# Rotary rows of the last attention packed into 128 partitions by POOL's transfers, and the norm's factor of the queries taken into the softmax

## The reference

```
def rmsnorm_2(x, g):
    y = x32 * lax.rsqrt(jnp.mean(x32 * x32, axis=-1, keepdims=True) + RMS_EPS)
    return (y * g.astype(jnp.float32)).astype(x.dtype)

def partial_rope(x, pos):                  # only the first 16 of 64 rows of a head turn
    x1, x2 = x32[..., :half], x32[..., half:ROT_DIM]
    rot = jnp.concatenate([x1 * cos - x2 * sin, x2 * cos + x1 * sin], axis=-1)
    return jnp.concatenate([rot.astype(x.dtype), x[..., ROT_DIM:]], axis=-1)

def swa_attention(q, k, v, sinks):
    s = jnp.einsum('bnqhgd,bnkhd->bnhgqk', qb, kw) * scale
    s = jnp.where(mask[None, :, None, None], s, NEG_INF)
    m = jnp.maximum(jnp.max(s, axis=-1, keepdims=True), sink)
    e = jnp.exp(s - m)
    denom = jnp.sum(e, axis=-1, keepdims=True) + jnp.exp(sink - m)
    o = jnp.einsum('bnhgqk,bnkhd->bqhgd', e / denom, vw)

h = rmsnorm_2(x, norm_g[1]); p = h @ swa_w_in
q, k = partial_rope(q, pos), partial_rope(k, pos)
y = swa_attention(q, k, v, swa_sinks) * silu(gate)
out = rmsnorm_2(x + y @ w_out, final_g)
```

## Time and profile before

| | |
|---|---|
| median of 3 executions | 2113.01 us (2110.41 to 2113.66) |
| profiled execution, its time | 2112.39 us |
| its span, first to last instruction | 2110.6 us |
| mean granted TensorE clock | 0.998 |
| busy: TensorE / VectorE / ScalarE / POOL | 2089.4 / 1618.0 / 1322.4 / 22.0 us |
| stretch of the last attention | from about 1780 us (end of `fo3`) to the end |

### The profile page before, as it was taken

The page is one execution under the profiler, slowest core; times in us unless marked ns, Lnnn a source line. Parts: engine busy times, 40 slices in busy tenths (PEclk is TensorE's granted clock), DMA queues, the critical chain, the costliest instruction groups (busy, mean ns, idle before and its releaser), DMA issues.

```text
span 2110.6 us, 35203 instructions
## 1 busy us (share of the span) xinstructions
PE 2089.4 (99%) x13756; PEld 1824.4 (86%) x13756; DVE 1618.0 (77%) x2935; ACT 1322.4 (63%) x2610; POOL 22.0 (1%) x42
## 2 busy tenths in 40 slices
PE   9999999999999999999999999999999999999998
PEld 8878888888898888888888888888888888988887
DVE  7899866787788888656888867777686777689874
ACT  6866447775676666544666666556566655567764
POOL 0000000000000000000000000000000000100000
PEclk9999999999999999999999999999999999999999
DMA  7544534665455555655555555555555555644464
GB/s 280 173 147 144 169 120 143 224 219 193 160 190 192 196 192 191 197 193 196 191 195 192 194 196 191 190 191 190 198 182 178 171 195 193 213 159 160 160 210 139
DMA packets 108325, 390.94 MB, mean 185 GB/s; under 512 B 12624, under 2 KB 12880, under 8 KB 107392
## 3 DMA queue, kind: packets, MB, share of 16 engines
q1 hardware_dynamic: 105264, 377.34, 54.0%
q0 software_dynamic: 2608, 11.04, 1.5%
q10 hardware_dynamic: 288, 0.32, 0.0%
HBM read 384.36 MB, written 2.13 MB: 183 GB/s over the span
## 4 chain that ended last, share of the span: by engine, by line
PE 91%; DVE 6%; ACT 2%; issue 1%; DMA 0%; SPq 0%; DVEq 0%; ACTq 0%
PE main L597 86%; PE two L597 4%; DVE W L1104 2%; PE two L600 1%; DVE gt L1104 1%; DVE GV L1110 0%; ACT W L1826 0%; ACT L1825 0%; DMA RAW<-ws 0%; ACT PPw L1826 0%; DVE GK L1110 0%; DVE PB L1104 0%; DVE GQ L1110 0%; DVE NTL L1104 0%; PE main L644 0%
## 5 line engine op out<-in xcount | busy, mean ns | idle before, releaser
L597 PE MATMUL main<-A,W 128*128 128x256 f32 (+2 forms) x7200 | 1249.6, 334 | 7.7 <-DVE W L1104 7.3
L1826 ACT ACTIVATE W<-RAW 128x512 fp32r<-128x512 f32 x1416 | 876.7, 627 | 589.6 <-PE main L597 583.7
L597 PEld LDWEIGHTS main<-A,W 128*128 128x128 f32 (+1 forms) x7200 | 1088.5, 188 | 161.6 <-DVE W L1104 10.6
L1104 DVE TENSOR_TENSOR W<-RAW,W 128x512 fp32r<-128x512 f32 x1416 | 956.3, 685 | 354.6 <-ACT W L1826 345.8
L597 PE MATMUL main<-H,W 128*128 128x512 f32 (+1 forms) x1408 | 239.7, 333 | 0.0
L597 PEld LDWEIGHTS main<-H,W 128*128 128x128 f32 x1408 | 212.2, 188 | 27.3
L597 PE MATMUL main<-B,W 128*128 128x512 f32 (+1 forms) x1216 | 197.9, 324 | 0.3 <-DVE B L1104 0.3
L597 PEld LDWEIGHTS main<-B,W 128*128 128x128 f32 x1216 | 177.3, 188 | 20.4 <-issue 0.5
L597 PE MATMUL main<-W,A 128*128 128x512 f32 (+1 forms) x672 | 150.2, 378 | 0.0
L597 PEld LDWEIGHTS main<-W,A 128*128 128x128 f32 x672 | 117.9, 188 | 22.4 <-issue 0.5
L597 PE MATMUL main<-W,B 128*128 128x512 f32 x384 | 88.2, 390 | 0.0
(11 more groups left out here) (329 smaller groups left out, 1359.9 us busy)
## 6 DMA issues: line engine op xcount, KB each, us to landing
RAW<-ws SPq DMA_DIRECT2D x707, 512.0 KB, 3.3
CB<-cscr POOLq DMA_DIRECT2D x4, 1024.0 KB, 5.3
XT<-xT POOLq DMA_DIRECT2D x4, 512.0 KB, 7.6
MS<-memT POOLq DMA_DIRECT2D x4, 512.0 KB, 10.0
xs<-xT SPq DMA_DIRECT2D x7, 256.0 KB, 8.3
out<-YT SPq DMA_DIRECT2D x7, 256.0 KB, 2.5
CST<-cst SPq DMA_DIRECT2D x1, 1272.0 KB, 7.5
VR<-WV POOLq DMA_DIRECT2D x16, 64.0 KB, 4.5
```

What stands on the lines that cost most here:

```text
L597: return e.matmul(o, l, r, start=start, stop=True, skip_group_check=True)
L1104: return e.tensor_tensor(o, a, b, op)
L1826: return e.activation(o, i, f, bias=bias, scale=scale, accum_out=accum)
```

## The change

- The keys (WK) are multiplied by RB in place, like other parts, at slot END["fo3"] + 13 on VectorE. ScalarE's `keys` copies them to KR 16 slots earlier than before (T_WROPE - 10, with T_WROPE one lower).
- The queries are not multiplied by their factor at all. The row maximum of the raw scores is multiplied by RT inside the maximum with the sink (two instructions of two columns in place of one of four, since RT differs by half), and the exponential takes RT as its scale.
- SP's 36 crosswise transfers, the zeroed ROT tiles and the 9 rotary parts of three 128x512 operations go. In their place: for the keys (r = 0) and each group of eight heads (r = 1 to 4) POOL gathers the 16 turning rows of the tiles' eight halves into one tile PQ of 128 partitions by 256 tokens, and the same rows crosswise into PV, by six transfers; VectorE multiplies PQ and PV by new tables and adds, three operations of 128x256; POOL brings PQ back by two transfers. TensorE's scores wait for that (s_rope) instead of rp_done. VectorE's part is at T_WROPE and T_QROPE[g] = END[wq g] + 6; POOL does its own when the semaphores allow, behind `values` in its list.

```diff
+    for r in range(16):
+        for base in (4 * r, 64 + 4 * r):
+            C[base:base + 4] = cos[r % 8]
+            S[base:base + 4] = sin[r % 8] if r >= 8 else -sin[r % 8]
...
-    if form_of(*_x) == "wide" and _x[0][:2] not in ("wo", "dn", "fo", "w2", "wk", "wq"):
+    if form_of(*_x) == "wide" and _x[0][:2] not in ("wo", "dn", "fo", "w2", "wq"):
...
+        elif _x[0] == "wkv":
+            _e = max(_e, END["fo3"] + 13)
...
-T_WROPE = ENDS["wkv", 0] + 17
-T_QROPE = [[ENDS[f"wq{g}", p] + (15 if (g, p) == (2, 1) else 10) for p in range(2)] for g in range(4)]
+T_WROPE = ENDS["wkv", 0] + 16
+T_QROPE = [END[f"wq{g}"] + 6 for g in range(4)]
...
-            def swap(r):
-                src, dst = wide_to(*ROPED[r]), ROT[r % 2]
...
-                for base in (0, 64):
-                    lower, upper = slice(base, base + 8), slice(base + 8, base + 16)
-                    e.dma_start(dst[lower, :, :], src[upper, :, :]).then_inc(s_rot[r % 2], 16)
-                    e.dma_start(dst[upper, :, :], src[lower, :, :]).then_inc(s_rot[r % 2], 16)
...
-                w.wait_ge(rp_done, 2 * g + 3)
+                w.wait_ge(s_rope, 32 * (g + 2))
...
-                    z = tt(h2(mx), h2(mx), bm(sink, 2), ALU.max)
+                    for t in range(2):
+                        m = mx[:, 2 * t:2 * t + 2]
+                        z = stt(m, m, RT[:, t:t + 1], sink, ALU.mult, ALU.max)
...
-            def rope(key, part, r):
-                yield
-                w.wait_ge(s_rot[r % 2], 64 * (r // 2 + 1))
-                v, d = ROT[r % 2][:], wide_to(key, part)
-                if r == 0:
-                    w.wait_ge(s_rb, 5)
-                    w.wait_ge(v_own, own(tt(ROPE, ROPE, bm(RB[:], 2), ALU.mult)))
-                tt(d, d, bm(ROPC, 2), ALU.mult)
-                t = own(tt(v, v, bm(ROPS, 2), ALU.mult))
+            def rope(r):
+                w.wait_ge(s_pack, 96 * (r + 1))
+                tt(PQ[:], PQ[:], ROPC, ALU.mult)
+                t = own(tt(PV[:], PV[:], ROPS, ALU.mult))
                 yield
                 w.wait_ge(v_own, t)
-                tt(d, d, v, ALU.add).then_inc(rp_done, 1)
+                tt(PQ[:], PQ[:], PV[:], ALU.add).then_inc(rp_done, 1)
...
-                        z = act(S[:, h, x0:x1], S[:, h, x0:x1], ACTF.Exp, bias=mx[:, n:n + 1], accum=dn[:, n:n + 1])
+                        z = act(S[:, h, x0:x1], S[:, h, x0:x1], ACTF.Exp, bias=mx[:, n:n + 1],
+                                scale=scales[:, j:j + 1] if scales is not None else 1.0, accum=dn[:, n:n + 1])
...
             def keys():
-                yield from ticks(5)
-                w.wait_ge(rp_done, 1)
+                w.wait_ge(s_scl, SCALED["wkv", 0])
...
-            def clear():
-                w.wait_ge(s_B, B_STAGE["f"] + 16)
-                for rot in ROT:
-                    z = e.memset(rot[:], 0.0)
-                z.then_inc(zeroed, 1)
-                yield
+            def rope(r):
+                if r == 0:
+                    w.wait_ge(s_kr, 8)
+                    tiles = KR
+                else:
+                    w.wait_ge(s_evac, CHUNK[f"wq{r - 1}", 1] + 1)
+                    w.wait_ge(s_rope, 32 * r)
+                    tiles = AQ[:, 4 * r - 4:4 * r, :]
+                for h in (0, 64):
+                    e.dma_start(PQ[h:h + 64, :], tiles[h:h + 16]).then_inc(s_pack, 16)
+                    e.dma_start(PV[h:h + 32, :], tiles[h + 8:h + 16]).then_inc(s_pack, 16)
+                    e.dma_start(PV[h + 32:h + 64, :], tiles[h:h + 8]).then_inc(s_pack, 16)
+                yield
+                w.wait_ge(rp_done, r + 1)
+                for h in (0, 64):
+                    e.dma_start(tiles[h:h + 16], PQ[h:h + 64, :]).then_inc(s_rope, 16)
...
-            parts += [(END["wkv"] + 1, values())]
+            parts += [(END["wkv"] + 1, values()), (T_WROPE - 5, rope(0))] + [(T_QROPE[g] - 5, rope(1 + g)) for g in range(4)]
```

More of the change, by code:

```diff
@@ L251 @@
         SCALING[_e].append(_x)
-ROPED = [("wkv", 0)] + [(f"wq{g}", p) for g in range(4) for p in range(2)]
-LOWED = {x: n + 1 for n, x in enumerate(x for x in KEYS if x in set(itertools.chain(ROPED, *SCALING)))}
+QUERIES = [(f"wq{g}", p) for g in range(4) for p in range(2)]
+LOWED = {x: n + 1 for n, x in enumerate(x for x in KEYS if x in set(itertools.chain(QUERIES, *SCALING)))}
 for _x in itertools.chain(*SCALING):
@@ L337, in program @@
         s_vr, wp_sum = sem("s_vr"), sem("wp_sum")
-        zeroed, rp_done, s_kr, s_rot = sem("zeroed"), sem("rp_done"), sem("s_kr"), sems("s_rot", 2)
+        zeroed, rp_done, s_kr, s_pack, s_rope = (sem(n) for n in ("zeroed", "rp_done", "s_kr", "s_pack", "s_rope"))
         s_g2, fin_y, fin_sq, fin_sum, fin_rs, fin_ve, fin_ac = (
@@ L1799, in vector_program @@
             parts += [(T_FO[n][p], residual("fo", n, p, "n1")) for n in range(4) for p in range(2)]
-            parts += [(T_WROPE, rope("wkv", 0, 0))]
-            parts += [(T_QROPE[g][p], rope(f"wq{g}", p, 1 + 2 * g + p)) for g in range(4) for p in range(2)]
+            parts += [(T_WROPE, rope(0))] + [(T_QROPE[g], rope(1 + g)) for g in range(4)]
             parts += [(T_SWA[g][p], swa(g, p)) for g in range(4) for p in range(4)]
@@ L2133, in forget, with exps @@
                 copy(CTN[0:32, :], banks[7][0:32, 0:256], scale=-1.0).then_inc(lf_ac, 1)
-            def exps(S, mx, dn, end=384):
+            def exps(S, mx, dn, end=384, scales=None):
                 for j, (x0, x1) in enumerate(((0, 128), (128, end))):
@@ L2166, in swa @@
                 w.wait_ge(wp_ve[lane], W_VE * i + 2)
-                exps(S, mx, dn, 256)
+                w.wait_ge(s_rt, 5)
+                exps(S, mx, dn, 256, RT)
                 act(sk, sk, ACTF.Exp).then_inc(wp_ac[lane], 1)
@@ L2180, in swa @@
                 if g == 3:
-                    w.wait_ge(rp_done, len(ROPED))
+                    w.wait_ge(s_rope, 160)
                 for qi in range(4):
@@ L2296, in scalar_program @@
             parts += [(T_FO[n][p], residual("fo", n, p, "n1")) for n in range(4) for p in range(2)]
-            parts += [(T_WROPE, keys())]
+            parts += [(T_WROPE - 10, keys())]
             parts += [(T_SWA[g][p], swa(g, p)) for g in range(4) for p in range(4)]
@@ L2383, in pool_program @@
             parts += [(END["gz1"], reload()), (T_MEM, mem()), (T_FF, forget())]
-            parts += [(END[f"fv{g}"], bias(g)) for g in range(4)] + [(END["fo0"], clear())]
-            parts += [(END["wkv"] + 1, values())]
+            parts += [(END[f"fv{g}"], bias(g)) for g in range(4)]
+            parts += [(END["wkv"] + 1, values()), (T_WROPE - 5, rope(0))] + [(T_QROPE[g] - 5, rope(1 + g)) for g in range(4)]
             interleave(parts, NH, lambda j: None)
```

13 lines of the change are left out of this document (1 added, 12 removed).

## The result

| | before | changed |
|---|---|---|
| median, executions | 2112.01 us, 7 | 2119.43 us, 7 (2116.60 to 2120.88) |
| ratio | | 1.0032 (1.0022 to 1.0041) |
| profiled execution, span | 2112.39, 2110.6 us | 2117.35, 2115.5 us |

What follows compares the result with a forecast made beforehand. TensorE, busy 2089.4 of 2110.6 us, bounds the kernel, so only its pauses count: -2.06 - 1.75 + 0.2 + 0.1 + 2.4 = -1.1 against 2112.39 gives 2111.3 us; range 2108.6 to 2115.6.

Steps and rivals of the forecast that it cites:

- first pause and its clock, residual: TensorE's wait for VectorE before 1918.24 goes, -2.06 us, its clock fall too, -1.75; later short pauses +0.2.
- maxima: In each of 16 score pairs one 128x4 operation becomes two of 128x2; +0.1 us, from the last pair.
- column scale: Exponentials taking their scale from a column instead of a constant: costed at nothing.
- late keys with clock: VectorE stands 7.7 us for keys packed behind VR; TensorE pauses until 1828.2, +2.4 us; a clock fall adds 1.75.
- Rival C: First pause stays, ScalarE's bunched exponentials being its cause: 2114.9 us, with the clock 2116.6; chance 0.08.
- at most 0.1 us in the tail: Upper bound given for the cost of the exponentials' scale column, at the kernel's end.
- VectorE still: After the first pause VectorE is what is late next, with row maxima queued behind that W; +0.2 us (0 to 0.6).
- four in ten: Chance given that the clock falls after the new pause near 1826, +1.75 us, making 2113.0 us.
- one in four brought a fall: Count of TensorE's earlier pauses followed by a clock fall, from which the chance of another fall was set.
- A: Packed keys landing within 2.1 us of the last start cause no pause, 2108.9 us; up to 3.4, 2110.2; chance 0.22.
- B: POOL's six issues behind VR held up by VectorE operations, 4.1 us more; pause 6.5 us, 2117.1 us; chance 0.08.
- the prediction's 15 us: Extra time for POOL's six issues if VectorE locks GpSimd out, sum near 2127; the trace's 536 ns speak against it.

Runs made afterwards that it cites:

- e6: Changed kernel with keys' transfers ahead of VR, constant exponential scale, queries' factor left out and the row maximum in one operation: 2108.35 us, ratio 0.9981.
- e4: The kernel with both edits: changed kernel with keys' transfers ahead of VR and constant exponential scale, queries' factor left out: 2109.26 us, ratio 0.9987.
- e3: Changed kernel with POOL's six transfers for the packed keys ahead of the 16 for VR: 2113.70 us, ratio 1.0008.
- e2: Changed kernel with a constant exponential scale and a column of ones in the row maxima, queries' factor left out: 2114.49 us, ratio 1.0010.

## Why the prediction was wrong

| term | predicted | from the runs |
|---|---|---|
| first pause and its clock, residual | -3.6 | -3.8 (e6: packing and the keys' earlier copies) |
| maxima | +0.1 | +0.7 to +1.3 |
| column scale | 0 | +4.2 to +4.9 |
| late keys with clock | +2.4 (4.15) | +5.2 to +5.7 |
| sum | -1.1 | +6.3 to +8.1; measured +7.4 |

That the sum meets the +7.4 proves little, since the runs from e6 by e4 and e3 to the changed kernel are a chain whose steps add up to it by themselves. What bears the last three terms is that each was measured twice, in two kernels, with nearly the same value; the first has one run and its trace.

**Bound and first pause: right.** VectorE's queue was the cause; the pause and the clock fall at 1918 are gone. Rival C is out: 1916 to 1920 has TensorE busy 3.91 of 4 us at clock 1.00, and between the pauses at 1900.25 and 1957.95 none is over 0.31 us.

**"Exponentials take their scale from a column instead of a constant; the bias already is a column, and I cost it at nothing": the main failure.** The sentence rested on no row: that one column was already read was taken to mean that a second is free, and the only bound was 0.1 us in the tail. The trace of before had the price. Its activations without a column took 0.19 us on 128x4 and 0.62 on 128x512, which makes some 0.30 us on 128x128, and the exponential with one column took 0.39: an estimate of 0.09 us for a column, or 64 x 0.09 = 6 us of ScalarE time for the second. The 93 ns of the Trainium skill, page "ScalarE: Activation LUTs", section "What ACT_TABLE_LOAD costs", give the same 64 x 0.093 = 6 us, an estimate too. What matters is where they stand. Two pairs' eight exponentials come close behind each other on ScalarE, with one high half between, ahead of high halves that VectorE waits for. ScalarE's timeline in the changed kernel, from the first of the eight to the high halves behind the last:

```profile
1941.69 0.49 ACT L1808 ACTIVATE PPw<-PPw,SM 128x128 f32<-128x128 f32 x1 [1.36 <-DVE SM L1094]
...
1946.25 1.65 ACT L1808 ACTIVATE W<-RAW 128x512 fp32r<-128x512 f32 x3
```

and in the kernel with both edits, at the same place of the program:

```profile
1935.15 0.41 ACT L1808 ACTIVATE PPw<-PPw,SM 128x128 f32<-128x128 f32 x1 [0.74 <-DVE SM L1094]
...
1938.97 1.66 ACT L1808 ACTIVATE W<-RAW 128x512 fp32r<-128x512 f32 x3
```

4.56 us against 3.82: the 0.74 more are eight times 0.09. The timeline of VectorE in the changed kernel behind that, ahead of the pause at 1957.95:

```profile
1946.89 0.69 DVE L1091 TENSOR_TENSOR W<-RAW,W 128x512 fp32r<-128x512 f32 x1 [1.83 <-ACT W L1808]
...
1957.20 1.90 DVE L1091 TENSOR_TENSOR W<-RAW,W 128x512 fp32r<-128x512 f32 x3
```

and in the kernel with both edits:

```profile
1939.61 0.69 DVE L1091 TENSOR_TENSOR W<-RAW,W 128x512 fp32r<-128x512 f32 x1 [1.33 <-ACT W L1808]
...
1949.93 1.29 DVE L1091 TENSOR_TENSOR W<-RAW,W 128x512 fp32r<-128x512 f32 x2
```

From the first W to the one TensorE waits for VectorE takes 10.31 us in the one and 10.32 in the other, so VectorE's own work there is not what differs; it starts 0.74 us later, behind ScalarE. TensorE's pause is 2.06 against 0.86 us; where the other 0.46 of the difference arises isn't shown. The "at most 0.1 us in the tail" fails too: the pauses from 1995 us on add up to 3.2 us in the changed kernel and with the keys first, and to 2.1 and 2.3 with the constant scale (e2, e4). The prediction asked of VectorE alone what is late next ("VectorE still") and took ScalarE's bunched exponentials up only as rival C, at the old place.

**The late keys: the mechanism right, the size too small.** Gap of VectorE 7.7 predicted, 7.85 in the trace; landing 4.5, 4.6; TensorE's pause 2.4, 2.50; issues 0.536, 0.52 to 0.58; clock fall four in ten, seen in both profiles with the late keys. Both that it fell and that the landing varies (4.9 us at most in one execution, 5.9 in another) lie on the dear side: from VD on 4.5 us in one profile (a pause of 2.5 and the clock) and 6.6 in the other (3.7 and the clock), and the medians at +5.2 to +5.7 between these two. The step that failed is the count of pauses, "one in four brought a fall", which left the 1.75 us out of the likeliest time; the pause of 1.75 us at 132 to 136 that it counted as one without a fall brings one in five of the ten traces. The changed kernel's median is 2.1 us above its profiled execution. A longer landing in most executions would give that, and so would a fall of the clock elsewhere, as the one near 136 us in five of the ten traces: the two slowest of the seven executions, 2120.66 and 2120.88 us, have the lowest mean granted clock, 0.996, against 0.998 in the profiled one, but 2119.6 us came with 0.999. The other executions have no trace, so the cause stays open.

**The maxima: undersized.** Two of 128x2 with a column factor take 218 ns each, not the 163 of the plain one, and from the start of the first to that of the next step it is 0.39 us (1996.93 to 1997.32), not 0.20. The prediction had the two 0.1 apart. That is 0.19 us for each of 16 pairs on VectorE, 3.0 us, of which 0.7 to 1.3 showed, neither of them clear of nothing alone.

**Rivals.** A is what the kernel with keys first made true for the keys (gap 0.52, no pause). B named a slower kernel, but its mechanism did not happen: POOL's issues never went over 0.6 us. The rule that the prediction cited from the Trainium skill, page "SBUF — State Buffer", section "SBUF: two separate sides", could not be seen at work here: it is about an operation in a two-port fast mode, and while POOL made the six issues VectorE ran nothing. With the keys first it ran W products beside them, and they took 0.52 to 0.57 us; but W products have two input tensors, and the same section says that such an operation has no two-port mode; the prediction's 15 us did not follow from the rule. The query packs (VectorE's gap of 2.27 us at the first group) and the write-backs cost TensorE nothing, as predicted. The range failed because the column scale had almost nothing in it: with 0 to 6 us for it the upper end would have been near 2121.6.

## What to carry to other kernels

A small operand that is "only another column" has a price per instruction, and a queue of short instructions multiplies it; before such a term is put at nothing, look for two rows that differ by the operand, as the activations with and without a column did here, and where there are none give it bounds. When a factor is moved from a few large operations into many small ones (tables into maxima and exponentials), look at which engine's burst it joins and who waits behind the burst. And a transfer that a busy engine will wait for belongs ahead of bulk transfers on the same queue: here the order of two list entries was worth 5.2 to 5.7 us. And one profiled execution can be off its median (here by up to 2.7 us), in part for reasons outside the edit: count from the last common instruction.

## What was not expected of the hardware

- A column as an exponential's scale, beside a column as its bias, costs about 90 ns on 128x128 (92 by busy time; 393 to 437 ns in the mean of a group half of which are exponentials).
- Pauses of TensorE of the same length are followed by a fall of the clock or not: 2.06 us before 1918.24 in the kernel before and 2.07 before 1954.92 with SP's pack, yes; 2.06 before 1957.95 in the changed kernel, 2.07 before 1953.66 with keys first, 2.08 and 2.09 in the kernel before with the column scale and with two maxima, no. The two longer ones, 2.50 and 3.72, were each followed by a fall. The shorter one near 135 us, 1.75 to 1.84, was in five of ten traces. A fall cost 1.4 to 1.8 us in a slice of 4. What decides it stays open.
- The same six transfers behind the same sixteen landed within 4.0 to 5.2 us in one execution and 5.2 to 6.1 in another.
